# The second layer's modulation on GpSimd and ACT, and the gate stores in small groups

## What is computed

```python
def _modulation(cvec, w_ada_l, b_ada_l):
    m = jax.nn.silu(cvec) @ w_ada_l + b_ada_l          # 1024 -> 6 * 1024
    return [t[:, None, :] for t in jnp.split(m, 6, axis=-1)]

def _layer(x, mods, params, attend):
    sh1, sc1, gt1, sh2, sc2, gt2 = mods
    h = _rmsnorm(x, g1) * (1 + sc1) + sh1
    a_in, a_b, a_c, p_in, q, k, v = jnp.split(h @ w_in_l, IN_SPLITS, axis=-1)
    y = concat([_short_conv(...), _multi_pool(...), attend(q, k, v)])
    x = x + gt1 * (y @ w_out_l)
    h = _rmsnorm(x, g2) * (1 + sc2) + sh2
    return x + gt2 * _peer(h, wq_l, sk_l, u_l, v_l)
```

## Time and profile before

| | us |
|---|---|
| median of three runs | 3071.91 |
| the profiled execution, its own time | 3072.93 |
| its span, first to last instruction | 3071.4 |
| PE busy | 2901.7 (94%) |
| DVE busy | 1812.9 (59%) |
| ACT busy | 1204.6 (39%) |
| GpSimd (POOL) busy | 10.0 (0%) |
| mean granted TensorE clock | 0.976 of full speed |

### The profile page before, as it was taken

How to read it: one execution, slowest core, us unless ns; L and a number is a source line. 1 busy time by engine, 2 the same in 40 slices (tenths; PEclk the granted TensorE clock), 3 DMA queues, 4 the chain that set the end, 5 groups by cost and what they waited for, 6 DMA issues and landing times.

```text
span 3071.4 us, 49237 instructions
## 1 busy us (share of the span) xinstructions
PE 2901.7 (94%) x16962; PEld 2658.9 (87%) x16962; DVE 1812.9 (59%) x4002; ACT 1204.6 (39%) x2024; POOL 10.0 (0%) x21
## 2 busy tenths in 40 slices
PE   6898999999997999999988989999999979999997
PEld 5877999999997888888778789999999978888886
DVE  3344377777863655555534445877778735555555
ACT  3243434344343444444332434443444434444443
POOL 0000000000000000000000000000000000000000
PEclk8999999999998999999988999999999989999999
DMA  6262353754847666666453524438457486656661
GB/s 271 103 234 93 124 170 123 231 187 130 269 132 263 246 222 214 237 225 217 154 220 140 197 83 145 157 127 264 148 173 239 133 272 250 222 214 235 225 219 69
DMA packets 256734, 581.68 MB, mean 189 GB/s; under 512 B 13024, under 2 KB 209888, under 8 KB 211616
## 3 DMA queue, kind: packets, MB, share of 16 engines
q1 hardware_dynamic: 255360, 571.81, 54.4%
q0 software_dynamic: 1184, 7.34, 0.6%
HBM read 475.82 MB, written 103.28 MB: 189 GB/s over the span
## 4 chain that ended last, share of the span: by engine, by line
PE 91%; DVE 2%; DMA 2%; SPq 2%; issue 1%; ACT 1%; ACTq 0%; DVEq 0%
PE ps L695 34%; PE ps L656 33%; PE ps L546 11%; PE ps L677 6%; PE ps L563 1%; SPq L363 1%; PE ps L511 1%; DMA wring<-in_w_ada_dram 1%; PE ps L621 1%; PE ps L638 1%; PE ps L489 1%; PE ps L591 1%; PE ps L610 1%; PE ps L590 0%; DMA act_scratch<-act_h 0%
## 5 line engine op out<-in xcount | busy, mean ns | idle before, releaser
L656 PE MATMUL ps<-h_lo,u_hi 128*128 128x384 f32 x2048 | 697.8, 341 | 47.7 <-DVE u_lo L1146 39.6
L656 PE MATMUL ps<-h_hi,u_lo 128*128 128x384 f32 x2048 | 688.6, 336 | 0.0
L656 PE MATMUL ps<-h_hi,u_hi 128*128 128x384 f32 x2048 | 688.1, 336 | 0.0
L1287 DVE TENSOR_TENSOR v_lo<-wring,v_hi 128x512 fp32r<-128x512 f32 x512 | 354.4, 692 | 447.0 <-ACT v_hi L920 447.0
L695 PE MATMUL ps<-v_hi,w_lo 128*128 128x512 f32 x1536 | 597.6, 389 | 0.0
L695 PE MATMUL ps<-v_hi,w_hi 128*128 128x512 f32 x1536 | 597.5, 389 | 0.0
L695 PE MATMUL ps<-v_lo,w_hi 128*128 128x512 f32 x1536 | 597.5, 389 | 0.0
L920 ACT CAST v_hi<-wring 128x512 fp32r<-128x512 f32 x512 | 317.9, 621 | 609.6 <-PE ps L695 609.5
L1146 DVE TENSOR_TENSOR u_lo<-wring,u_hi 128x1024 fp32r<-128x1024 f32 x256 | 312.6, 1221 | 246.2 <-ACT u_hi L877 242.5
L656 PEld LDWEIGHTS ps<-h_lo,u_hi 128*128 128x128 f32 x2048 | 387.5, 189 | 53.3 <-DVE u_lo L1146 44.8
L656 PEld LDWEIGHTS ps<-h_hi,u_hi 128*128 128x128 f32 x2048 | 387.3, 189 | 0.0
(11 more groups left out here) (162 smaller groups left out, 2969.7 us busy)
## 6 DMA issues: line engine op xcount, KB each, us to landing
wring<-in_u_t_dram SPq DMA_DIRECT2D x128, 1024.0 KB, 5.6
wring<-in_v_t_dram SPq DMA_DIRECT2D x128, 1024.0 KB, 4.9
wring<-in_w_ada_dram SPq DMA_DIRECT2D x48, 1024.0 KB, 5.1
act_scratch<-act_h SPq DMA_DIRECT2D x256, 192.0 KB, 5.7
gate_scratch<-g_all SPq DMA_DIRECT2D x48, 1024.0 KB, 5.9
gate<-gate_scratch SPq DMA_DIRECT2D x64, 768.0 KB, 6.3
act<-act_scratch SPq DMA_DIRECT2D x64, 768.0 KB, 7.9
wring<-in_w_in_dram SPq DMA_DIRECT2D x20, 1024.0 KB, 5.4
```

Source lines behind the costliest of these rows:

```text
L656: last = nc.tensor.matmul(ps[:, 6 + s % 2, 0:T], u[:, s % 2, k], hx[:, k], start=(k == 0 and n == 0), stop=(k == KC - 1 and n == 2))
L1287: V.tensor_tensor(v_lo[:, n % 4], wring[:, n // G].rearrange("p k n -> p (k n)") [:, (n % G) * 512:(n % G + 1) * 512], v_hi[:, n % 4].bitc ...
```

## The change

Three things are done.

1. The gate stores of a token block are spread otherwise. Of the first two token blocks, three, three and two pieces go out in three turns of u loads, instead of four and four in two. Of the third, one pair of hidden stores goes first, then three pieces, then V tiles, hidden stores and the loads of groups 0 and 1, and the other five pieces one, one and three behind later hidden stores.
2. The modulation of the second layer leaves PE, and its 24 tiles leave SP's stream. `next_modulation` on GpSimd loads both condition vectors to all partitions and the second layer's `w_ada`, turned so that a partition holds the 1024 inputs of an output (24 loads of 1 MB, two buffers), and multiplies: 96 products of 128x1024. ACT makes the silu of the condition at V unit 16 of the first layer, and from unit 32 on sums a product every second unit (a Copy with an accumulated output), so the last at unit 222. GpSimd may be two products ahead of ACT's sums. It adds the bias and makes `gs` when all are summed; the second layer's norms wait for that (`next_mods_rdy`).
3. The loop over the layers is written out on every engine, and on ACT the first layer's V units too.

SP at the end of the hidden stage: what stands behind the last gates of the third token block, in the kernel before (`act_h` are the hidden values, `g_all` the gates).

The diff, cut to its core:

```diff
-W_IN0 = N_ADA1
-W_ADA2 = W_IN0 + N_IN
-W_OUT0 = W_ADA2 + N_ADA2
-W_WQ0 = W_OUT0 + N_OUT
-W_SK0 = W_WQ0 + N_WQ
-W_PER = W_SK0 + 2
+N_MOD = 24
+MOD_UNIT = 32
+W_IN0 = (N_ADA1, 0)
+W_ADA2 = (W_IN0[0] + N_IN, None)
+W_OUT0 = (W_ADA2[0] + N_ADA2, N_IN)
+W_WQ0 = tuple(n + N_OUT for n in W_OUT0)
+W_SK0 = tuple(n + N_WQ for n in W_WQ0)
+W_PER = tuple(n + 2 for n in W_SK0)
...
+GATE_PIECES = {0: (0, 1, 2), 1: (3, 4, 5), 2: (6, 7)}
+TAIL_PIECES = {2: (3,), 3: (4,), 4: (5, 6, 7)}
...
+    def mods_wait(eng, l, which):
+        if l == 0:
+            eng.wait_ge(mods_rdy.sem, which + 1)
+        else:
+            eng.wait_ge(next_mods_rdy.sem, 1)
...
-        with sp.Fori(0, DEPTH) as l:
-
-            for n in range(W_PER):
-                for first, count, ada in ((0, N_ADA1, 0), (W_ADA2, N_ADA2, N_ADA1)):
-                    if first <= n < first + count:
-                        tile = w_ada[l, n - first + ada]
-                for first, count, src in ((W_IN0, N_IN, w_in), (W_OUT0, N_OUT, w_out), (W_WQ0, N_WQ, w_q)):
+        for l in range(DEPTH):
+
+            for n in range(W_PER[l]):
+                for first, count, ada in ((0, N_ADA1, 0), (W_ADA2[0], N_ADA2, N_ADA1)):
+                    if l == 0 and first <= n < first + count:
+                        tile = w_ada[n - first + ada]
...
-            def more_u(i, gates_of=None, piece=0, acts=True):
+            def more_u(i, gates_of=None, pieces=(), acts=True):
                 for s in range(WR):
 
                     sp.wait_ge(ulo_rdy.sem, ulo_rdy.at(l, 0) + (i * (2 * WR) + 2 * (s + 1 - WR)))
                     load_u(i * WR + s, s)
                     if acts or s:
                         store_acts(i, s)
-                    if gates_of is not None:
+                    if s < len(pieces):
 
                         sp.wait_ge(ulo_rdy.sem, ulo_rdy.at(l, 0) + (i * (2 * WR) + 2 * (s + 1 - WR) + 1))
-                        store_gates(gates_of, piece + s)
+                        store_gates(gates_of, pieces[s])
 
             more_u(1, acts=False)
             more_u(2)
-            with sp.Fori(0, TB - 1) as tb:
-                for turn in range(3, TB_TURNS + 1):
-                    more_u(tb * TB_TURNS + turn)
-
-                sp.wait_ge(gq_evac.sem, gq_evac.at(l, 0) + (tb + 1) * (NQ // TB))
-                more_u(tb * TB_TURNS + (TB_TURNS + 1), tb, 0)
-                more_u(tb * TB_TURNS + (TB_TURNS + 2), tb, WR)
-            for turn in range((TB - 1) * TB_TURNS + 3, NB // 8):
-                more_u(turn)
+            for turn in range(3, NB // 8):
+                tb, at_ = divmod(turn - TB_TURNS - 1, TB_TURNS)
+                if tb >= 0 and at_ == 0:
+                    sp.wait_ge(gq_evac.sem, gq_evac.at(l, (tb + 1) * (NQ // TB)))
+                    sp.sem_inc(sp_passed.sem, 1)
+                more_u(turn, tb, GATE_PIECES.get(at_, ()) if tb >= 0 else ())
 
             sp.wait_ge(gq_evac.sem, gq_evac.at(l, NQ))
-            for piece in range(PIECES):
+            sp.sem_inc(sp_passed.sem, 1)
+            store_acts(NB // (2 * WR), 0)
+            for piece in range(3):
...
-                store_acts(NB // (2 * WR), n)
+                if n:
+                    store_acts(NB // (2 * WR), n)
+                for piece in TAIL_PIECES.get(n, ()):
+                    store_gates(TB - 1, piece)
...
+        def next_modulation():
+
+            for sig in g_st:
+                pool.wait_ge(sig.sem, sig.at(0, 16 * TB))
+            for sig in act_st:
+                pool.wait_ge(sig.sem, sig.at(0, 16 * (2 * G // AR)))
+            pool.dma_start(c_b[:].rearrange("p v k -> p (v k)"), c_rows.to_broadcast([P, 2 * D])) \
+                .then_inc(cb_ld.sem, 16)
+
+            def load_mod(n):
+                pool.dma_start(mod_w[:, n % 2].rearrange("p r k -> p (r k)"), w_mod[n]).then_inc(mod_ld[n % 2].sem, 16)
+
+            load_mod(0)
+            load_mod(1)
+            pool.wait_ge(cb_rdy.sem, 1)
+            for n in range(N_MOD):
+                pool.wait_ge(mod_ld[n % 2].sem, 16 * (n // 2 + 1))
+                for m in range(4 * n, 4 * n + 4):
+                    if m >= 2:
+                        pool.wait_ge(mod_sum.sem, m - 1)
+                    nc.gpsimd.tensor_tensor(mod_p[:, m % 2], mod_w[:, n % 2, m // 2 % 2], c_b[:, m % 2], ALU.mult) \
+                        .then_inc(mod_mul.sem, 1)
+                if n + 2 < N_MOD:
+                    pool.wait_ge(mod_mul.sem, 4 * n + 4)
+                    load_mod(n + 2)
+            ch = Chain(pool, mod_ch, 0, 3)
+            pool.wait_ge(mod_sum.sem, 4 * N_MOD)
+            ch.then(nc.gpsimd.tensor_tensor(mods[1][:], mods[1][:],
+                                            vec_all[:, 1, 0:6 * KC].unsqueeze(2).to_broadcast([P, 6 * KC, 2]), ALU.add))
+            for which, (scale, gain) in enumerate(((SC1, ROW_G1), (SC2, ROW_G2))):
+                last = nc.gpsimd.tensor_scalar(gs[1][:, which], mods[1][:, scale:scale + KC], 1.0, None, ALU.add)
+            ch.then(last)
+            for which, (scale, gain) in enumerate(((SC1, ROW_G1), (SC2, ROW_G2))):
+                last = nc.gpsimd.tensor_tensor(gs[1][:, which], gs[1][:, which],
+                                               vec_all[:, 1, gain:gain + KC].unsqueeze(2).to_broadcast([P, KC, 2]),
+                                               ALU.mult)
+            ch.then(last)
+            ch.close()
+            pool.sem_inc(next_mods_rdy.sem, 1)
+        for l in range(DEPTH):
...
+            if l == 0:
+                for n in range(N_ADA1):
+                    modulation(n, n, (6,))
+                modulation_turned(0, (6,))
...
-                if n < N_ADA2:
-                    modulation(W_ADA2 + n, n, (4, 7))
-                if n == ADA_TURN:
+                if l == 0 and n < N_ADA2:
+                    modulation(W_ADA2[0] + n, n, (4, 7))
+                if l == 0 and n == ADA_TURN:
                     modulation_turned(1, (4, 7))
...
+                if l == 0:
+                    at_ = i * (4 * G) + n
+                    m, odd = divmod(at_ - MOD_UNIT, 2)
+                    if at_ == MOD_UNIT // 2:
+                        act.wait_ge(cb_ld.sem, 16)
+                        nc.scalar.activation(c_b[:], c_b[:], ACT.Silu).then_inc(cb_rdy.sem, 1)
+                    if not odd and 0 <= m < 4 * N_MOD:
+                        act.wait_ge(mod_mul.sem, m + 1)
+                        nc.scalar.activation(mod_p[:, m % 2], mod_p[:, m % 2], ACT.Copy,
+                                             accum_out=mods[1][:, m // 2, m % 2:m % 2 + 1]).then_inc(mod_sum.sem, 1)
+
+            output_units(act, unit_step, looped=l > 0)
```

More of the change, by code:

```diff
@@ L67 @@
 N_SPLIT = SP_WQ0 + 2 * N_WQ
-assert W_PER % WR == 0 and U_PER % WR == 0 and V_PER % WR == 0
-FILLS = (W_PER + U_PER + V_PER) // WR
+assert all(n % WR == 0 for n in W_PER) and U_PER % WR == 0 and V_PER % WR == 0
+FILLS = (W_PER[0] + U_PER + V_PER) // WR
 ADA_TURN = 18
@@ L285, in build @@
     y_st = S("y_st", 0)
+    cb_ld = S("cb_ld", 0)
+    cb_rdy = S("cb_rdy", 0)
+    mod_ld = [S(f"mod_ld{i}", 0) for i in range(2)]
+    mod_mul = S("mod_mul", 0)
+    mod_sum = S("mod_sum", 0)
+    mod_ch = S("mod_ch", 0)
+    next_mods_rdy = S("next_mods_rdy", 0)
     dve_passed = S("dve_passed", 0)
@@ L316, in s_bank, with output_units @@
         return (0, 1, 6)[n % 3]
-    def output_units(eng, unit_step):
+    def output_units(eng, unit_step, looped=True):
         for n in range(4 * G):
             unit_step(0, n, False)
-        with eng.Fori(1, NG // 2 - 1) as i:
-            for n in range(4 * G):
-                unit_step(i, n, False)
+        if looped:
+            with eng.Fori(1, NG // 2 - 1) as i:
+                for n in range(4 * G):
+                    unit_step(i, n, False)
+        else:
+            for i in range(1, NG // 2 - 1):
+                for n in range(4 * G):
+                    unit_step(i, n, False)
         for n in range(4 * G):
@@ L493, in _ @@
         pe.wait_ge(const_ld.sem, 16)
-        with pe.Fori(0, DEPTH) as l:
+        for l in range(DEPTH):
             pe.wait_ge(silu_rdy.sem, 1)
@@ L524, in modulation_turned @@
                 last.then_inc(ada_tr.sem, 1)
-            for n in range(N_ADA1):
-                modulation(n, n, (6,))
-            modulation_turned(0, (6,))
+            if l == 0:
+                for n in range(N_ADA1):
+                    modulation(n, n, (6,))
+                modulation_turned(0, (6,))
             def columns_split(M):
@@ L629, in _ @@
             column_blocks(SP_WQ0, HP, pq_mm, pq_evac, 2)
-            sk = [tile_in(W_SK0 + i).rearrange("p k n -> p (k n)") for i in range(2)]
+            sk = [tile_in(W_SK0[l] + i).rearrange("p k n -> p (k n)") for i in range(2)]
             def route_scores(tb):
@@ L766, in _ @@
             .then_inc(silu_rdy.sem, 1)
-        with act.Fori(0, DEPTH) as l:
+        for l in range(DEPTH):
             act.wait_ge(x_ld.sem, 16)
@@ L979, in gains @@
```

(10 more changed lines are left out.)

88 lines of the change are left out of this document (50 added, 38 removed).

## The result

The changed kernel takes 3130.99 us (median of four runs, 3127.56 to 3132.83) against 3071.64 us for the kernel before on the same chip: a ratio of 1.0194 [1.0178, 1.0211], 1.9% slower. The forecast was 3028 us, 44 us faster. The profiled execution has a span of 3125.6 us against 3071.4.

The account below looks back on a forecast made before the run. PE was taken to bound the kernel almost everywhere, bar three places. Gate stores 22, second layer's start 11, attention 14, less 3 for added V-stage work, make 44 us off 3072.93; with runs' median 1.0 lower, 3028 us, range 3009 to 3062.

Parts of the forecast that it names:

- All this costs 0 as long as GpSimd delivers a product each 4.08 us: First layer's V stage: added ACT, DMA and GpSimd work costs nothing; product taken as 2.0 us, 3 us added for first meetings.
- the turns: Rival, first layer's V stage: DVE and GpSimd take turns, 2 to 50 us lost, time 3035 to 3062; chance 25%.
- The product becomes the bound: Rival, first layer's V stage: products set PE's pace, 4.88 us period, 77 us lost, 3105 us; chance 9%.
- The estimate of 45 us: First layer's V stage: growth if the skill's shared read port lock and its 2.25 us product both held.
- Gate stores: End of hidden stage: hidden stores issued sooner gain 9 us in first layer, 13 in second; bounds 8 and 38.
- Start of the second layer: Before its projection: 9.0 us from modulation tiles gone, 2 from loop jumps gone; gain 11, bounds 8 and 13.
- Attention: Second layer's attention: PE loses tiles and transposes worth 18.0 us, 4 lost to exposed latency; gain 14, bounds 9 and 18.
- This rival: Second layer's attention: PE's clock stays low without the tiles, some 30 us lost, 3058 us; chance 3%.

Follow-up runs that it names:

- the run with the sum first: The changed kernel with ACT's sum moved ahead of the cast of `w_hi`; 3070.76 us, ratio 0.999.
- the fastest version: Changed kernel with products on DVE, silu at unit 24, sums from unit 40, group 2 loaded before the last three gate pieces, group 3 loaded earlier; 3018.91 us.
- the run with the sums spread out: The run with the sum first, with a sum at every 7/3 units instead of every 2; 3040.24 us, ratio 0.989.

## Why the prediction was wrong

**The step that failed** is "All this costs 0 as long as GpSimd delivers a product each 4.08 us", with its condition "if GpSimd and DVE work side by side". They don't. The product was bounded well, at 1.0 to 2.4 us, and measured 2.39; the choice of 2.0 and of side by side was where it went wrong: a cost put at 3 us measured 93. The terms of the turns were all in the rival: DVE's 2.3 us per two units, the product at its upper end, both in turn. The experiments split the loss of the V stage, against the 504.9 us of the run with DVE's products, in two. 32 us (536.9 - 504.9) are the turns: 2.3 + 2.1 us against 4.08, 96 times 0.34. The other 61 us (597.9 - 536.9) are the loop, which no part of the prediction had: the held `v_lo` delays `w`, ACT's `w_hi` waits for `w`, and the sum that releases the next product stands behind `w_hi`. The rows on ACT's order in the diff showed this; I asked whether ACT's work fits (2.80 of 4.08 us, and it does), not what each of its instructions waits for.

**The rivals.** "The product becomes the bound" had the right sign and place, with 9%, and 3105 us; its period of 4.88 us was measured as 5.09. By its own argument ACT's casts stand behind the sum. It lacked the step back from DVE to ACT that makes the circle. "Turns" at 25% and up to 3062 is what the run with the sum first shows, at 3071. More than half of the chance, 55%, went to side by side without a row for it; with no row on either side the 2.4 us end and the turns needed more than 34% together.

The Trainium skill, "SBUF — State Buffer", section "Who interferes with whom", has the lock, and the trace agrees: `v_lo` 2.48 us beside a product, 0.69 beside a memset. It does not agree for the GpSimd instruction with one input: the Trainium skill has the hold for the whole of any that reads SBUF, and there `v_lo` took 1.06 us beside 2.77. The estimate of 45 us by it and by the Trainium skill's "GPSIMD Engine Reference", section 3.1, rests on 2.25 us for a product (half of what that page has for an addition of 2048 float32; measured 2.39) and on the turns alone, for which the run with the sum first shows 32 us.

**Gate stores**, taken as 9 + 13. The second layer gained 8.1. In the first the gain was 0.4 wherever GpSimd's loads were issued beside group 2's (575.4 against 575.0 with the products on DVE): of the 10.1 that the grouping gives alone, 7.4 went to the loads, which I had put at 4, and the rest is 1.4 us ahead of the V stage and 0.9 in it, of which no run shows the cause. The mechanism held: V began 35 us behind the start of the last eight blocks instead of 53, PE waited at unit 10, and in the second layer that wait was 7.4 us instead of 6. But group 2's load was issued 53 us behind the last gates (948.1 to 1001.20), not 50.5 (952.5 to the forecast's 1003; its own 48 us would end at 1000.5), against 56.5 before:

```profile
987.87 6.59 SPq L391 DMA_DIRECT2D gate_scratch<-g_all  x3
1001.20 0.41 SPq L436 DMA_DIRECT2D gate<-gate_scratch  x1
```

The last three pieces go out only at 987.87, and nothing else is in the queue while SP waits for them to land. The fastest version puts group 2 ahead of them, and the two layers' stretches fall to 562.3 and 557.4 us.

**Start of the second layer**, taken as 11, measured 14.2. Beside the 9 us of the tiles that leaves 5 for the written-out loops, not 2. PE's sums now follow the last transposes without the 3.49 us of idle time:

```profile
1619.45 1.17 PE L785 MATMUL ps<-cst,acc 128*128 128x128 f32 x6 [0.28 <-DVE x L1088]
1620.46 5.33 PE L561 MATMUL ps<-h,cst 128*128 128x384 f32 x16
```

**Attention**, taken as 14, measured 9.8 (9.6 in the run with the sums spread out); 6.5 to 6.7 in five others, among them those with DVE's products, with memsets and with half products, and 4.3 in the fastest version and in the run with the sum first, all by the same stretch and the same code. Two things were short. PE waits longer for the probabilities, 8.7 us instead of 5.2 (waits of PE in the stage, before and then after):

```profile
PE ps L610 <- DVE pr L1127: 5.2, 4, 3.1
```

```profile
PE ps L684 <- DVE pr L1213: 8.7, 6, 3.1
```

And the clock. The earlier trace rows had 1.00 with less than half of 6 us busy, and I took from that that it stays up. In the mean over the stage it was 0.95 before, 0.87 in the changed kernel, and 0.79 in the fastest version:

```profile
1739.00:1804.00 65.00, 55.19 (x280) 42.26 (x280) 31.11 (x102) 34.03 (x101) 0.23 (x1) 0.87 0.03 9
```

```profile
1636.00:1708.00 72.00, 61.99 (x288) 47.28 (x289) 32.18 (x104) 35.12 (x103) 0.73 (x1) 0.79 0.03 8
```

At 0.50 for the low level that is 17 us low in the one (65 x 0.13 / 0.5) and 30 in the other, and the two differ by 5.5 us. In the rows of the changed kernel (1742 to 1754) the clock falls in the slices behind the gap, not in it, so that a high number in the gap itself is no evidence. This rival, with 3% and 30 us, was real in part: it took some 4 us in the changed kernel and 10 in the fastest version, if all that is missing from 14 is put down to it. An estimate from the three groups of runs says nearly the same: between the first and the last lie 5.5 us of time and some 14 us of low clock, so 0.4 us for each, and the two versions had some 10 and 23 us more at the low level than the kernel before, which makes 4 and 9. Why the clock falls sooner in one run than in another with the same code, no run shows.

**Without the lock** the time would have been 3038 us, not 3028: four versions that take the lock or most of its length away gave 3038.0 to 3039.1 (one execution each for three of them; the four of the run with DVE's products lie within 7 us). They are 34 to 36 us faster than the kernel before on their chips, so the terms beside the lock were some 10 us too hopeful together. The gates of both layers, 0.4 + 8.1, lie at the lower bound of 8, the start's 14.2 above its bound of 13, and the attention inside its 9 to 18 in the changed kernel but below in the runs with 6.7 or less.

## What to carry to other kernels

Work given to an idle engine is not free because that engine is idle: it can stop a busy one. Here one GpSimd instruction of two SBUF inputs stopped DVE for 2.1 of its 2.4 us, while DVE could have done the same product in 1.22 us of its own idle time. Check a new cross-engine chain for circles, by asking who waits for each instruction that stands behind the new wait, not only whether each engine's sum of work fits the period. And when the price of a resource is bounded only from rows far off, work the sum out at the bad end first: 2.4 us and turns were both in the prediction, and together they were the result.
